# The MLP's first two blocks split by ScalarE and VectorE, and a final norm that follows the last block row by row

## The chip, the cores and the metric

The kernel runs on one core of one Trainium2 chip, in fp32. The metric is device time in microseconds of one execution; lower is better. The median of three runs of the kernel before is 1596.93 us (1596.89 to 1600.69).

## The reference

One layer of a hybrid decoder: a state-space branch and a retention branch whose gated sum goes through `w_out` to the residual, then an MLP with a squared relu, then a last RMS norm. The change touches only what is computed from here on (x, z and h are 1024 x 1024, `w_up` is 1024 x 4096, `w_down` is 4096 x 1024), and every root of an RMS norm:

```python
    z = rmsnorm(h, norm_mlp[l])
    h = h + jnp.square(jax.nn.relu(z @ w_up[l])) @ w_down[l]
return rmsnorm(h, norm_final)
```

## The kernel before, in words

Each fp32 product is made of three matmuls of reduced precision: both operands are split in a rounded part `_hi` and a rest `_lo`, and `three` (L625 to L629) issues hi x hi, hi x lo and lo x hi. So every weight and activation has to be cast (hi) and subtracted (lo) by some engine before TensorE (PE) can use it. Weights come by SP's queue into `stage`, two buffers of 128 x 1024; nothing is loaded into a buffer until its last content has been split.

The 4096 hidden columns are worked off in 16 blocks of 256. The first two (`plain_block`, f = 0 and 1) are plain: four up tiles of 24 matmuls (two column blocks q for each half of the rows) and then 16 down tiles of 6 matmuls, each of them one row chunk c by one half j of the columns, added by VectorE (DVE) from the four banks of `acc` to `h_res` (L2044). The other 14 (`win_block`) use seven half-size up products into `aux` in place of eight, with sums of quarters of the activations (`s1_sum` to `s4_sum`, made by DVE in `form_s1` to `form_s4`, split by ScalarE (ACT) and DVE in `lo_s`) in the gaps of the plain blocks.

What sets the order is each engine's own program and the counters between engines. In a plain block ACT takes relu of up tile n (L1358) and only then makes the `hid_hi` of tile n - 1; DVE squares `relu` (L2055), waits for `hid_hi`, makes `hid_lo` (L1421), and does the sums between these steps. Down tile n waits until tile n - 4 has been added to `h_res` (`out_free`), since there are four banks; the fifth down tile also waits for the last two `hid_lo`. GpSimd (POOL) splits the weights of both plain blocks (`plain_split`, L549 and L551): those of f = 1 once the four up tiles of f = 0 are done. Then it makes the first pieces of block 0's transformed weights as soon as the up tiles of f = 1 are done.

The last block's down products go, as in all blocks, first through all eight rows with j = 0 and then with j = 1 (`DOWN_ORDER` is 4, 5, 6, 7, 0, 1, 2, 3), so a row of `h_res` is complete only in the second half. ACT sums its squares (L1404), DVE takes the roots of rows 0 to 3 together, then of 4 and 5, then of 6 and 7 (`last_rstd`, `rstd`), and multiplies with the root and `nf` (`last_norm`, L2151) in rows 0, 2, 4, 6, 7; rows 1, 3, 5 are scaled by ACT (L1410) and multiplied with `nf` by POOL (L620). SP stores the rows in order, 512 KB each. `nf` lies in `stage` and is loaded (L467) when the last weights have been split. In `rstd` the root is a shift of the bits and three Newton steps on a column or a few; every dependent step waits for the one before (`link`). A root of one column uses TENSOR_SCALAR with two pointer operands, one of several columns TENSOR_TENSOR.

## Time and profile before

| | us |
|---|---|
| median of three runs | 1596.93 |
| the profiled execution | 1595.84 |
| its span in the profile | 1594.0 |
| PE busy | 1516.0 (95%) |
| DVE busy | 955.1 (60%) |
| POOL busy | 434.1 (27%) |
| ACT busy | 292.9 (18%) |
| TensorE's mean granted clock | 0.984 |

In the 40 slices of the profile (39.85 us each) PE stands at 9 tenths from the third slice on but for four slices at 8, one at 6 and the last at 4. The 6 is the slice from 916.6 to 956.4 us, where the plain blocks lie; the last one holds the final norm. In the chain that ended last PE has 84%, DVE 10%, SP's queue 2%. A shown matmul duration of 0.39 us is not its share of the engine, since matmuls overlap: what counts is the distance between starts.

### The profile page before, as it was taken

To read this page: it belongs to the slowest core of one execution; us is meant where nothing else is said; L and a number is where in the kernel's file an instruction comes from. 1 tells how busy PE (TensorE), PEld (TensorE's weight loads), DVE (VectorE), ACT (ScalarE), POOL (GpSimd) and SP (SyncE) were. 2 spreads that over 40 slices of the span, in tenths; PEclk is the share of its full clock that TensorE was granted. 3 is DMA by queue.
4 is the path that set the end of the run, shared out by engine and by line. 5 is a ranking of instruction groups with operands and counts; after the bars stand their busy time and mean duration, and the time that the engine had idled before them with its cause. 6 is when DMAs were issued, how large, how long until landed. Compare 5 with 4: busy or idle time off the path is not lost.

```text
span 1594.0 us, 21227 instructions
## 1 busy us (share of the span) xinstructions
PE 1516.0 (95%) x7440; PEld 1267.6 (80%) x7440; DVE 955.1 (60%) x1928; ACT 292.9 (18%) x569; POOL 434.1 (27%) x363
## 2 busy tenths in 40 slices
PE   5898999899999999999999968999999999999994
PEld 4786888789898989878888756888888888888884
DVE  6688656553565646575516686655555555555557
ACT  4121111210222222241102212111111111111113
POOL 1210101321010101105323133344444444444442
PEclk9999999999999999999999989999999999999997
DMA  5423434354110101104442010111111111111113
GB/s 165 121 93 99 124 98 125 106 192 146 47 54 26 53 26 41 39 27 137 160 158 66 1 53 1 53 53 53 53 53 53 53 53 46 47 52 53 53 40 118
DMA packets 105604, 119.17 MB, mean 75 GB/s; under 512 B 23504, under 2 KB 73808, under 8 KB 105552
## 3 DMA queue, kind: packets, MB, share of 16 engines
q1 hardware_dynamic: 74704, 78.49, 16.1%
q10 hardware_dynamic: 30848, 40.00, 8.0%
q8 instruction: 32, 0.52, 0.1%
q14 instruction: 20, 0.16, 0.0%
HBM read 96.57 MB, written 20.97 MB: 74 GB/s over the span
## 4 chain that ended last, share of the span: by engine, by line
PE 84%; DVE 10%; SPq 2%; ACT 1%; ACTq 1%; DMA 1%; issue 1%; POOL 0%; DVEq 0%
PE acc L627 21%; PE acc L629 20%; PE acc L628 20%; PE aux L629 6%; PE aux L627 6%; PE aux L628 6%; SPq L393 1%; PE aux L871 1%; PE aux L865 1%; PE aux L874 1%; DMA stage<-in_w_in 1%; PE aux L758 1%; ACTq L1127 1%; DVE tb L1734 1%; PE aux L764 0%
## 5 line engine op out<-in xcount | busy, mean ns | idle before, releaser
L2044 DVE TENSOR_TENSOR h_res<-h_res,acc 128x512 f32<-128x512 f32 x256 | 170.8, 685 | 109.5 <-PE acc L629 108.3
L627 PE MATMUL acc<-dw_hi,hid_hi 128*128 128x512 f32 x512 | 201.1, 393 | 19.7 <-DVE h_res L2044 19.7
L629 PE MATMUL acc<-dw_hi,hid_lo 128*128 128x512 f32 x512 | 200.6, 392 | 0.0
L628 PE MATMUL acc<-dw_lo,hid_hi 128*128 128x512 f32 x512 | 200.6, 392 | 0.0
L627 PE MATMUL acc<-w_hi,z_hi 128*128 128x256 f32 (+1 forms) x512 | 189.0, 369 | 0.0
L627 PE MATMUL acc<-z_hi,w_hi 128*128 128x512 f32 x448 | 179.5, 401 | 9.7 <-DVE z_lo L1421 5.0
L502 POOL CAST w_hi<-stage 128x1024 fp32r<-128x1024 f32 x44 | 48.6, 1121 | 494.3 <-PE acc L629 323.4
L628 PE MATMUL acc<-z_lo,w_hi 128*128 128x512 f32 x448 | 176.5, 394 | 0.0
L629 PE MATMUL acc<-z_hi,w_lo 128*128 128x512 f32 x448 | 176.4, 394 | 0.0
L629 PE MATMUL acc<-w_hi,z_lo 128*128 128x256 f32 (+1 forms) x512 | 173.0, 338 | 0.0
L628 PE MATMUL acc<-w_lo,z_hi 128*128 128x256 f32 (+1 forms) x512 | 172.8, 338 | 0.0
L627 PEld LDWEIGHTS acc<-dw_hi,hid_hi 128*128 128x128 f32 x512 | 97.0, 190 | 41.7 <-DVE h_res L2044 21.0
L2093 DVE TENSOR_TENSOR tmp<-tmp,aux 128x512 f32<-128x512 f32 x84 | 57.3, 683 | 103.4 <-PE aux L629 103.4
L629 PEld LDWEIGHTS acc<-dw_hi,hid_lo 128*128 128x128 f32 x512 | 96.9, 189 | 20.3
L628 PEld LDWEIGHTS acc<-dw_lo,hid_hi 128*128 128x128 f32 x512 | 97.1, 190 | 20.0
L627 PEld LDWEIGHTS acc<-z_hi,w_hi 128*128 128x128 f32 x448 | 85.4, 191 | 30.3 <-DVE z_lo L1421 5.8
L629 PEld LDWEIGHTS acc<-w_hi,z_lo 128*128 128x128 f32 x512 | 97.0, 189 | 10.8
L628 PEld LDWEIGHTS acc<-w_lo,z_hi 128*128 128x128 f32 x512 | 97.4, 190 | 8.1
L627 PEld LDWEIGHTS acc<-w_hi,z_hi 128*128 128x128 f32 x512 | 97.2, 190 | 8.2
L629 PEld LDWEIGHTS acc<-z_hi,w_lo 128*128 128x128 f32 x448 | 85.3, 190 | 18.4
L628 PEld LDWEIGHTS acc<-z_lo,w_hi 128*128 128x128 f32 x448 | 85.5, 191 | 17.2
L582 POOL TENSOR_TENSOR t_lo<-stage,t_hi 128x512 fp32r<-128x512 f32 x70 | 91.9, 1313 | 5.6
(300 smaller groups left out, 2839.5 us busy)
## 6 DMA issues: line engine op xcount, KB each, us to landing
stage<-in_w_up SPq DMA_DIRECT2D x32, 512.0 KB, 3.9
stage<-in_w_down SPq DMA_DIRECT2D x32, 512.0 KB, 3.4
stage<-in_w_in SPq DMA_DIRECT2D x28, 512.0 KB, 4.4
gate_dram<-gate_t ACTq DMA_DIRECT2D x32, 256.0 KB, 2.0
x_in<-in_x SPq DMA_DIRECT2D x8, 512.0 KB, 8.2
stage<-in_w_in SPq DMA_DIRECT2D x32, 128.0 KB, 2.7
stage<-in_w_in SPq DMA_DIRECT2D x16, 256.0 KB, 3.2
gb_t<-gate_dram ACTq DMA_DIRECT2D x16, 256.0 KB, 3.0
```

The lines of the kernel that those rows point to most:

```text
L393: sp.dma_start(coef[rows, i, :], t[name][0, gp::2, :].rearrange("g p -> p g"), allow_slow_non_contiguous=True).then_inc(lam_in, 16)
L502: nc.gpsimd.tensor_copy(dst_hi, stage[:, s, :]).then_inc(hi_pool, 1)
L582: nc.gpsimd.tensor_tensor(t_lo[:, slot, :, :], src, t_hi[:, slot, :, :].bitcast(F32), ALU.subtract)\
L627: nc.tensor.matmul(out, s_hi, m_hi_, start=first, stop=False)
L628: nc.tensor.matmul(out, s_hi, m_lo_, start=False, stop=False)
L629: return nc.tensor.matmul(out, s_lo, m_hi_, start=False, stop=last)
L758: nc.tensor.matmul(aux[:, 2 + gp, q * P:(q + 1) * P], toep[:, gp * QP + q, :], u_blk[:, 2 * q + gp, :], start=(q == 0), stop=False)
L865: nc.tensor.matmul(aux[:, 3, 0:DV], kvk[:, c % 2, :], vv[:, c % 2, :], start=True, stop=True)
L871: mm = nc.tensor.matmul(aux[:, 2, 0:DV], prob[:], vv[:, c % 2, :], start=True, stop=(c == 0))
L874: mm = nc.tensor.matmul(aux[:, 2, 0:DV], qkt[:, 0, :], state[:], start=False, stop=True)
L2044: V.tensor_tensor(h_res[:, c, hs], h_res[:, c, hs], acc[:, p % 4, :], ALU.add)\
L2093: V.tensor_tensor(dst, src, aux[:, bank, :], ALU.add).then_inc(taken, 1)
```

## The change

It has four parts.

- **Second block's weights.** The weights of f = 1 are cast by ACT (`second_hi`) and subtracted by DVE (`second_lo`), at fixed places of their programs, with the counters `second_cast` and `second_ready`; POOL splits only those of f = 0. SP's loads that followed POOL's splits follow `second_ready`.
- **Order in the plain blocks.** ACT makes `hid_hi` of tile n right after its relu. DVE makes the sums in another order: `form_s3(1)` moves to f = 1, the two `lo_s` of s3 move from ahead of the down products to among them.
- **The last block.** Its down products go row by row, both halves of a row one after the other; `dw` of j = 1 is split before the last two hidden tiles. DVE only adds, and takes roots in pairs of rows with the instructions of the two interleaved (`pair_rstd`); POOL multiplies rows 0 to 6 with `nf`, ACT scales them; DVE does row 7 in two halves, one stored by SP and one by ACT's queue. PE's and ACT's loops end one block earlier, with the last block written out behind them.
- **Roots.** Every root takes its first guess from the bits of the halved negative value, which saves one instruction.

```diff
+ROOT_BITS = 1597463007.0 - 2.0 ** 22 - 2.0 ** 30
...
+                    if f == 1:
+                        sp.wait_ge(second_ready, j + 1)
+                        sp.dma_start(stage[:, j, :].rearrange("p (k c) -> p k c", k=FT),
+                                     w_dn[:, FT * f:FT * f + FT, j * HALF:(j + 1) * HALF]).then_inc(raw[j], 16)
+                    else:
+                        load(LD_MLP + 4 * f + 2 + j, w_dn[:, FT * f:FT * f + FT, j * HALF:(j + 1) * HALF])
...
-                        sp.wait_ge(w_ready, LD_MLP + 4 * N_PLAIN - 1 + i)
+                        sp.wait_ge(second_ready, 3 + i)
...
-            for p, c in enumerate(DOWN_ORDER):
-                if p % 2 == 0 or p == NCH - 1:
-                    sp.wait_ge(f_done, (p + 1) // 2 + 1)
-                else:
-                    sp.wait_ge(f_done_pool, p // 2 + 1)
+            for p, c in enumerate(DOWN_ORDER[:-1]):
+                sp.wait_ge(f_scaled, p + 1)
                 sp.dma_start(out_rows[:, c, :], h_res[:, c, :]).then_inc(stored, 16)
-            sp.wait_ge(stored, 16 * NCH)
+            sp.wait_ge(f_done, 1)
+            sp.dma_start(out_rows[:, DOWN_ORDER[-1], 0:HALF], h_res[:, DOWN_ORDER[-1], 0:HALF]).then_inc(stored, 16)
+            sp.wait_ge(stored, 16 * (NCH + 1))
...
-            for f in range(N_PLAIN):
-                pool.wait_ge(out_ready, OUT_MLP - 8 if f == 0 else OUT_MLP + 4)
-                for i in range(2):
-                    n = LD_MLP + 4 * f + i
-                    plain_split(n, flat(pw_hi[:, KH * i:KH * i + KH, :]), flat(pw_lo[:, KH * i:KH * i + KH, :]), n + 1)
-                for j in range(2):
-                    n = LD_MLP + 4 * f + 2 + j
-                    if f > 0:
-                        pool.wait_ge(out_ready, OUT_MLP + PLAIN_OUT * (f - 1) + 4 + 8 * (j + 1))
-                    plain_split(n, flat(dw_hi[:, j, :, :]), flat(dw_lo[:, j, :, :]), n + 1)
+            pool.wait_ge(out_ready, OUT_MLP - 8)
+            for i in range(2):
+                n = LD_MLP + i
+                plain_split(n, flat(pw_hi[:, KH * i:KH * i + KH, :]), flat(pw_lo[:, KH * i:KH * i + KH, :]), n + 1)
+            for j in range(2):
+                n = LD_MLP + 2 + j
+                plain_split(n, flat(dw_hi[:, j, :, :]), flat(dw_lo[:, j, :, :]), n + 1)
...
-            for p, c in enumerate((DOWN_ORDER[1], DOWN_ORDER[3], DOWN_ORDER[5])):
-                pool.wait_ge(f_scaled, p + 1)
+            for p, c in enumerate(DOWN_ORDER[:-1]):
+                pool.wait_ge(f_ss, p + 1)
...
+            def down_rows(n0, h0, waits, order):
+
+                for p, c in enumerate(order):
+                    for j in range(2):
+                        down_tile(n0, 2 * p + j, p, c, j, h0, waits)
...
-                    if n >= 1:
-                        hidden_hi(4 * f + n - 1, relu[:, (n - 1) % 2, :], (n - 1) % FT, (n - 1) // FT)
-                hidden_hi(4 * f + 3, relu[:, 1, :], 1, 1)
+                    hidden_hi(4 * f + n, relu[:, n % 2, :], n % FT, n // FT)
+
+            def second_hi(i, dst):
+
+                act.wait_ge(raw[i % 2], 16 * (LD_RET // 2 + HEADS + (LD_MLP - LD_PB) // 2 + 2 + i // 2 + 1))
+                nc.scalar.activation(dst, stage[:, i % 2, :], ACT.Copy).then_inc(second_cast, 1)
 
             plain_block(0)
+            for i in range(2):
+                second_hi(i, pw_hi[:, KH * i:KH * i + KH, :].rearrange("p k c -> p (k c)"))
             for u in range(2):
                 s_hi(3 + u, s2_hi[:, 2 * u:2 * u + 2, :], s2_sum[:, 2 * u:2 * u + 2, :])
+            for j in range(2):
+                act.wait_ge(out_ready, OUT_MLP + 4 + 8 * (j + 1))
+                second_hi(2 + j, dw_hi[:, j, :, :].rearrange("p k c -> p (k c)"))
+            plain_block(1)
...
+                s_hi(5 + 2 * u, s3_hi[:, 2 * u:2 * u + 2, :], s3_sum[:, 2 * u:2 * u + 2, :])
...
+                    if last and i == 1:
+                        dw_hi_part(g, 1)
+                if not last:
+                    dw_hi_part(g, 1)
...
+            def square_f(p):
+                act.wait_ge(out_free, OUT_WIN + 16 * (N_WIN - 1) + 2 * p + 2)
                 if p >= 1:
                     act.wait_ge(f_ss, p)
-                nc.scalar.activation(h_junk[:], h_res[:, c, :], ACT.Square, accum_out=ss2[:, p:p + 1])\
+                nc.scalar.activation(h_junk[:], h_res[:, DOWN_ORDER[p], :], ACT.Square, accum_out=ss2[:, p:p + 1])\
                   .then_inc(f_ss, 1)
-                for s, after in ((1, 4), (3, 5), (5, 7)):
-                    if p == after:
-                        r = DOWN_ORDER[s]
-                        act.wait_ge(f_rstd, 1 if s < 4 else 2)
-                        nc.scalar.activation(h_res[:, r, :], h_res[:, r, :], ACT.Copy, scale=rs2[:, s:s + 1])\
-                          .then_inc(f_scaled, 1)
+
+            def scale_f(p):
+                act.wait_ge(f_done_pool, p + 1)
+                act.wait_ge(f_rstd, p // 2 + 1)
+                nc.scalar.activation(h_res[:, DOWN_ORDER[p], :], h_res[:, DOWN_ORDER[p], :], ACT.Copy,
+                                     scale=rs2[:, p:p + 1]).then_inc(f_scaled, 1)
+
+            for p in range(4):
+                square_f(p)
+            scale_f(0)
+            scale_f(1)
+            square_f(4)
+            square_f(5)
+            scale_f(2)
+            scale_f(3)
+            square_f(6)
+            square_f(7)
+            scale_f(4)
+            scale_f(5)
+            scale_f(6)
+            act.wait_ge(f_done, 2)
+            act.dma_start(out_rows[:, DOWN_ORDER[-1], HALF:D], h_res[:, DOWN_ORDER[-1], HALF:D]).then_inc(stored, 16)
...
-                bits, (tmp, m, y, y2) = rs_bits[:, 0:w], [rs_tmp[:, i, 0:w] for i in range(4)]
-                V.tensor_scalar(m, a, -0.5 / width, -0.5 * EPS, ALU.mult, ALU.add)
-                link(V.tensor_scalar(tmp, a, 1.0 / width, EPS, ALU.mult, ALU.add))
-                link(V.tensor_scalar(bits, tmp.bitcast(I32), 1, None, ALU.arith_shift_right))
-                link(V.tensor_scalar(y.bitcast(I32), bits, -1.0, 1597463007.0, ALU.mult, ALU.add))
+                bits, (m, y, y2) = rs_bits[:, 0:w], [rs_tmp[:, i, 0:w] for i in range(3)]
+                link(V.tensor_scalar(m, a, -0.5 / width, -0.5 * EPS, ALU.mult, ALU.add))
+                link(V.tensor_scalar(bits, m.bitcast(I32), 1, None, ALU.arith_shift_right))
+                link(V.tensor_scalar(y.bitcast(I32), bits, -1.0, ROOT_BITS, ALU.mult, ALU.add))
...
-                    if f == 1 and n < 2:
-                        form_s4(n)
-                    if f == 1 and n >= 2:
+                    if f == 1 and n == 0:
+                        second_lo(3, dw_lo[:, 1, :, :], dw_hi[:, 1, :, :])
+                        form_s4(0)
+                    if f == 1 and n == 1:
+                        form_s3(1)
+                    if f == 1 and n == 2:
+                        form_s4(1)
+                    if f == 1 and n == 3:
                         for u in range(2):
-                            lo_s(2 * n + u - 3, (s2_hi, s3_hi)[n - 2], (s2_lo, s3_lo)[n - 2],
-                                 (s2_sum, s3_sum)[n - 2], u)
+                            lo_s(1 + u, s2_hi, s2_lo, s2_sum, u)
                 for j, p in down(n0 + 4, range(NCH)):
-                    if f == 0 and j == 0 and p == 3:
+                    if f == 0 and j == 0 and p in (1, 3):
+                        ks = slice(KH * (p // 2), KH * (p // 2) + KH)
+                        second_lo(p // 2, pw_lo[:, ks, :], pw_hi[:, ks, :])
+                    if f == 0 and (j, p) == (0, 7):
                         form_s2(1)
-                    if f == 0 and (j, p) in ((0, 7), (1, 3)):
-                        form_s3(j)
-                    if f == 1 and j == 0 and p in (2, 5):
-                        lo_s1(p // 4)
+                    if f == 0 and (j, p) == (1, 3):
+                        form_s3(0)
+                    if f == 0 and (j, p) == (1, 6):
+                        second_lo(2, dw_lo[:, 0, :, :], dw_hi[:, 0, :, :])
+                    if f == 1 and j == 0 and p in (1, 3):
+                        lo_s(3 + p // 2, s3_hi, s3_lo, s3_sum, p // 2)
+                    if f == 1 and j == 0 and p in (5, 7):
+                        lo_s1(p // 2 - 2)
                     if f == 1 and j == 1 and p in (2, 5):
                         lo_s(7 + p // 4, s4_hi, s4_lo, s4_sum, p // 4)
+
+            def second_lo(i, dst, hi):
+                dve.wait_ge(second_cast, i + 1)
+                V.tensor_tensor(dst.rearrange("p k c -> p (k c)"), stage[:, i % 2, :],
+                                hi.rearrange("p k c -> p (k c)").bitcast(F32), ALU.subtract).then_inc(second_ready, 1)
...
+                if last:
+                    dw_lo_part(g, 1)
...
+            def last_rows(n0):
+
+                for p, c in enumerate(DOWN_ORDER):
+                    for j in range(2):
+                        i = 2 * p + j
+                        dve.wait_ge(out_ready, n0 + i + 1)
+                        hs = slice(j * HALF, (j + 1) * HALF)
+                        V.tensor_tensor(h_res[:, c, hs], h_res[:, c, hs], acc[:, i % 4, :], ALU.add).then_inc(out_free, 1)
+                    if p in (2, 4, 6):
+                        pair_rstd(p - 2)
+                pair_rstd(6)
+                dve.wait_ge(f_rstd, 4)
+                c = DOWN_ORDER[-1]
+                for j in range(2):
+                    hs = slice(j * HALF, (j + 1) * HALF)
+                    V.scalar_tensor_tensor(out=h_res[:, c, hs], in0=h_res[:, c, hs], scalar=rs2[:, 7:8], in1=nf[:, hs],
+                                           op0=ALU.mult, op1=ALU.mult).then_inc(f_done, 1)
+
+            def pair_rstd(p):
+
+
+                dve.wait_ge(f_ss, p + 2)
+                two = [(ss2[:, i:i + 1], rs2[:, i:i + 1], rs_bits[:, i - p:i - p + 1],
+                        [rs_tmp[:, k, i - p:i - p + 1] for k in range(3)]) for i in (p, p + 1)]
+                (a0, d0, b0, (m0, y0, t0)), (a1, d1, b1, (m1, y1, t1)) = two
+                V.tensor_scalar(m0, a0, -0.5 / D, -0.5 * EPS, ALU.mult, ALU.add)
+                link(V.tensor_scalar(m1, a1, -0.5 / D, -0.5 * EPS, ALU.mult, ALU.add))
+                V.tensor_scalar(b0, m0.bitcast(I32), 1, None, ALU.arith_shift_right)
+                link(V.tensor_scalar(b1, m1.bitcast(I32), 1, None, ALU.arith_shift_right))
+                V.tensor_scalar(y0.bitcast(I32), b0, -1.0, ROOT_BITS, ALU.mult, ALU.add)
+                link(V.tensor_scalar(y1.bitcast(I32), b1, -1.0, ROOT_BITS, ALU.mult, ALU.add))
+                for step in range(3):
+                    V.tensor_scalar(t0, y0, y0, m0, ALU.mult, ALU.mult)
+                    link(V.tensor_scalar(t1, y1, y1, m1, ALU.mult, ALU.mult))
+                    V.tensor_scalar(d0 if step == 2 else y0, t0, 1.5, y0, ALU.add, ALU.mult)
+                    ins = V.tensor_scalar(d1 if step == 2 else y1, t1, 1.5, y1, ALU.add, ALU.mult)
+                    ins.then_inc(f_rstd, 1) if step == 2 else link(ins)
```

## Rows read from the trace of the kernel before

**Rows 1.** Windows: PE, PEld, DVE, ACT, POOL busy (instructions), granted clock, DMA share, GB/s.
```profile
1043.00:1570.00 527.00, 527.00 (x2324) 436.04 (x2323) 303.41 (x427) 71.19 (x98) 227.46 (x224) 1.00 0.16 51
1570.00:1575.00 5.00, 3.84 (x17) 2.84 (x16) 4.59 (x16) 2.62 (x5) 0.84 (x1) 1.00 0.00 0
```

**Rows 2.** Timeline of PE: start, duration, engine, line, operation [idle before <-releaser].
```profile
928.01 0.80 PE L627 MATMUL acc<-dw_hi,hid_hi 128*128 128x512 f32 x1 [10.32 <-DVE h_res L2044]
...
943.26 0.50 PE L627 MATMUL acc<-dw_hi,hid_hi 128*128 128x512 f32 x1 [1.99 <-DVE h_res L2044]
...
984.23 0.80 PE L627 MATMUL acc<-dw_hi,hid_hi 128*128 128x512 f32 x1 [7.43 <-DVE h_res L2044]
```

**Rows 3.** Timeline of DVE in the first plain block.
```profile
908.00 0.69 DVE L1421 TENSOR_TENSOR hid_lo<-tmp,hid_hi 128x512 fp32r<-128x512 f32 x1 [4.09 <-ACT hid_hi L1039]
...
909.86 1.23 DVE L2004 TENSOR_TENSOR s_part<-m_lo 128x1024 f32<-128x1024 f32 x1
...
914.32 3.41 DVE L2003 TENSOR_TENSOR s_sum<-m_hi 128x1024 f32<-128x1024 f32 x1
...
919.74 3.25 DVE L2005 TENSOR_TENSOR s_sum<-s_sum,s_part 128x1024 f32<-128x1024 f32 x1
...
927.28 2.47 DVE L2044 TENSOR_TENSOR h_res<-h_res,acc 128x512 f32<-128x512 f32 x4
```

**Rows 4.** Timeline of POOL in the same stretch, the last of four operations.
```profile
918.70 3.20 POOL L551 TENSOR_TENSOR pw_lo<-stage,pw_hi 128x1024 fp32r<-128x1024 f32 x1
```

**Rows 5.** Windows behind idle stretches of PE, columns as in rows 1; then its timeline.
```profile
928.00:932.40 4.40, 4.39 (x10) 3.51 (x11) 4.37 (x6) 0.67 (x2) 0.00 (x0) 0.50 0.00 0
943.26:947.26 4.00, 4.00 (x18) 3.31 (x19) 3.97 (x5) 0.44 (x1) 0.00 (x0) 1.00 0.04 14
703.70:707.30 3.60, 3.60 (x10) 2.83 (x9) 3.25 (x13) 0.00 (x0) 0.00 (x0) 0.53 0.00 0
285.00:289.00 4.00, 4.00 (x49) 3.76 (x49) 0.00 (x0) 0.00 (x0) 0.79 (x1) 1.00 0.44 130
...
703.37 0.50 PE L627 MATMUL acc<-z_hi,w_hi 128*128 128x512 f32 x1 [2.59 <-DVE z_lo L1421]
```

**Rows 6.** Timeline of DVE in the second plain block, before its down products.
```profile
973.27 3.85 DVE L2030 TENSOR_TENSOR s_lo<-s_sum,s_hi 128x1024 fp32r<-128x1024 f32 x2
...
979.74 3.84 DVE L2030 TENSOR_TENSOR s_lo<-s_sum,s_hi 128x1024 fp32r<-128x1024 f32 x2
983.50 1.87 DVE L2044 TENSOR_TENSOR h_res<-h_res,acc 128x512 f32<-128x512 f32 x3
```

**Rows 7.** Timeline of DVE: the steps of one root of one column.
```profile
9.10 0.15 DVE L1435 TENSOR_SCALAR rs_tmp<-ss 128x1 f32<-128x1 f32 x1
9.16 0.14 DVE L1436 TENSOR_SCALAR rs_tmp<-ss 128x1 f32<-128x1 f32 x1
...
9.72 0.27 DVE L1442 TENSOR_SCALAR rs_tmp<-rs_tmp 128x1 f32<-128x1 f32 x1
10.03 0.21 DVE L1443 TENSOR_SCALAR rs_tmp<-rs_tmp 128x1 f32<-128x1 f32 x1
```

**Rows 8.** Timelines of ACT and DVE in the final norm; the last is SP's landing time.
```profile
1565.08 1.06 ACT L1404 ACTIVATE h_junk<-h_res 128x1024 bf16<-128x1024 f32 x1 [9.97 <-DVE h_res L2044]
...
1588.38 2.48 DVE L2151 SCALAR_TENSOR_TENSOR h_res<-h_res,rs,stage 128x1024 f32<-128x1024 f32 x2
...
stage<-in_norm_final SPq DMA_DIRECT2D x1, 512.0 KB, 3.6
```

**Rows 9.** Timelines of POOL and DVE, where both are at work.
```profile
846.18 2.39 POOL L551 TENSOR_TENSOR dw_lo<-stage,dw_hi 128x1024 fp32r<-128x1024 f32 x1
...
846.59 0.27 DVE L1442 TENSOR_SCALAR rs_tmp<-rs_tmp 128x1 f32<-128x1 f32 x1
...
1578.24 2.34 POOL L620 TENSOR_TENSOR h_res<-h_res,stage 128x1024 f32<-128x1024 f32 x1 [0.69 <-ACT h_res L1410]
...
1578.28 2.32 DVE L1446 TENSOR_TENSOR rs_tmp<-rs_tmp 128x2 f32<-128x2 f32 x1
```

More of the change, by code:

```diff
@@ L964, in _, with down_tile @@
                         turn_z2(c - 2)
+            def down_tile(n0, i, p, c, j, h0, waits):
+                pe.wait_ge(out_free, n0 + (i - 3))
+                if j == 0 and p % 4 == 0:
+                    pe.wait_ge(lo_done, h0 + 2 + p // 2)
+                if p == 0:
+                    pe.wait_ge(*waits[j])
+                for q in range(FT):
+                    mm = three(acc[:, i % 4, :], hid_hi[:, q, c * P:(c + 1) * P],
+                               hid_lo[:, q, c * P:(c + 1) * P], dw_hi[:, j, q, :], dw_lo[:, j, q, :],
+                               q == 0, q == FT - 1)
+                mm.then_inc(out_ready, 1)
             def down(n0, h0, waits, order):
@@ L1001, in plain_block, with win_block @@
                         mm.then_inc(out_ready, 1)
-                down(n0 + 4, SP_HID + 4 * f, [(w_ready, LD_MLP + 4 * f + 3 + j) for j in range(2)], range(NCH))
-            def win_block(g, first):
+                down(n0 + 4, SP_HID + 4 * f, [(w_ready, LD_MLP + 3 + j) if f == 0 else (second_ready, 3 + j) for j in range(2)], range(NCH))
+            def win_block(g, first, last=False):
                 a = {"A11": (m_hi[:, 0:KH, 0:HALF], m_lo[:, 0:KH, 0:HALF]),
@@ L1025, in win_block @@
                     mm.then_inc(prod, 1)
-                down(g * 16 + OUT_WIN, g * 4 + (SP_HID + 4 * N_PLAIN), [(dn_ready, g * 2 + (1 + j)) for j in range(2)],
-                     DOWN_ORDER)
+                (down_rows if last else down)(g * 16 + OUT_WIN, g * 4 + (SP_HID + 4 * N_PLAIN),
+                                              [(dn_ready, g * 2 + (1 + j)) for j in range(2)], DOWN_ORDER)
             for f in range(N_PLAIN):
@@ L1376, in _, with win_block @@
                   .then_inc(s_cast, 1)
[L1378 removed]
+            def win_block(g, last=False):
                 h0 = g * 4 + 4 * N_PLAIN
@@ L2143, in last_rstd @@
[L2143 to L2152 removed]
+                for _ in down(g * 16 + OUT_WIN, DOWN_ORDER):
+                    pass
```

61 lines of the change are left out of this document (16 added, 45 removed).

## The prediction

> **What bounds the kernel now.** I read the page first: TensorE (PE) is busy for 95% of the span and has 84% of the chain that ended last, so only time in which PE stands or runs slowly counts. The windows by stage come next. From 1043 to 1570 us, in the transformed blocks, PE starts 2324 matmuls in 527.0 us without a gap and at full clock, one per 0.227 us; a down tile of six thus takes 1.36 us and an up tile of 24 takes 5.45 us [rows 1]. Nothing is to be had there. PE's timeline then shows what the change can reach. In the first plain block PE stands 10.32 us ahead of its fifth down tile and 1.99 us further on; in the second block it stands 7.43 us at the same place [rows 2]. Each time the releaser is the addition to `h_res` by VectorE (DVE). The last place is behind PE's end: 3.84 of the 5 us from 1570 on are busy, so PE ends at about 1573.8 and 20.2 us of span follow [rows 1].
>
> DVE's timeline says why the addition is late. It has not begun adding: it starts at 927.28 and goes through four at once, 0.61 us each [rows 3]. Ahead of that lie the sums. One operation of 128x1024 takes 1.23 us while POOL rests, but the three of `form_s1(1)` take from 914.32 to 922.99, that is 8.67 us [rows 3], just while POOL splits the second block's weights, its own subtraction lengthened to 3.20 us [rows 4]. And `hid_lo` of tile 1 waited 4.09 us for a cast that ScalarE (ACT) gives only after the next tile's relu [rows 3].
>
> **First plain block.** Without POOL's splits `form_s1(1)` takes 3 x 1.25 = 3.75 us: 4.9 us go. ACT's cast right after its relu brings `hid_lo` of tile 1 from 908.0 to about 904.6: its wait of 4.09 shrinks to the 0.7 us that one cast and its handing over take. What follows in DVE's order (one sum, square, cast, `hid_lo`) moves up by the same 3.3 us. The additions start 8.2 us earlier, and the stall of 10.32 becomes 2.1. Late next is again the first addition, now behind `form_s2(0)`.
>
> TensorE's clock: behind the 10.32 us of idle time it was granted at 0.50, the lower level of 1.2 GHz, and ten matmuls took 4.40 us in place of 2.27 [rows 5], so 2.1 us more are lost. Behind 1.99 us of idle time it stayed at full speed [rows 5]. At the length that remains the trace has both: the matmuls behind the wait at 285 us ran at full clock, those behind 2.59 us of idle time at 703 us had 0.53 for ten matmuls, a loss of 3.60 - 2.27 = 1.3 us [rows 5]. I take no fall here.
>
> The splits move to ACT and DVE: four casts of about 1.1 us on ACT, which is idle most of the time, and four subtractions of 1.23 us on DVE. Three of these and two sums (2.5 and 3.75 us) share the 16 down tiles with 16 additions of 0.61: 9.8 + 3.7 + 6.2 = 19.7 us of DVE work under 21.8 us of PE work. With four banks an addition may be about 3.5 us late before PE waits; the longest insertion is `form_s3(0)`, 3.75 us, with DVE less than a microsecond behind then, so at most some tenths. The 1.99 us stall goes, since the second `form_s3` has left this block, and so does a wait of 0.3 at its end. The second block's first weights are ready in the middle of these tiles, some 12 us before PE wants them. Behind ACT's waits are queued only its casts for s2, which nobody needs before the second block. SP's loads wait for `second_ready` in place of POOL: 3 to 4 us of landing against more than 15 of cover. Gain of the first block: 8.2 + 2.1 + 2.0 + 0.3 = 12.6 us.
>
> **Second plain block.** Before, the square of the last hidden tile waited for two `lo_s` that took 3.85 us [rows 6], and POOL was making its first pieces all the time; two more `lo_s` (3.84) stood between `hid_lo` and the additions at 983.50 [rows 6]. The first two are moved among the down tiles; in their place the last operation of `form_s4(1)` reaches into the stretch with POOL, about 1.9 us. POOL starts its pieces at the same point relative to PE, so the latter two `lo_s` stay slow. The stall goes from 7.43 to 3.6 us. Its bounds: if DVE suffers nothing from POOL it would be 0.7, if everything is lengthened as in the first block (8.67 for 3.75) 5.5. I take 3.6, since the nearest rows are the same operations beside the same POOL work [rows 6]. After that much I let the clock fall as before, so its cost stays. The `lo_s` between the down tiles cost a few tenths at full clock and nothing while PE is slow. Gain 3.8 us, bounds 1.9 and 8.2 (the latter with the clock kept). Together 16.4 us.
>
> **The last block.** Row by row, a row of `h_res` is complete every 2.73 us rather than in the second half, so squares, roots, products and stores start about 8 us earlier. What bounds is DVE. Its pair of roots is 18 operations of one column. The trace shows two independent ones 0.06 us apart, and a dependent one 0.31 behind an operation with two pointers [rows 7]; an interleaved pair of two pointer operations is not in it. Bounds: with 0.06 throughout it is 2.9 us, with no overlap at all 4.5. I take 3.4, adding to 0.06 the 0.12 by which an operation with pointers is longer than one without [rows 7]. In two rows DVE then has 4 x 0.61 + 3.4 = 5.8 us of work in PE's 5.45, so it falls a little behind, and the third root stands ahead of the last two additions.
>
> I laid the four programs side by side from these durations: square 1.06 + 0.2 and its reading [rows 8], scaling 1.15, POOL's product 2.34 [rows 9]. `nf` is requested when the last `dw` is split, at about 1552.8, and lands 3.6 us later [rows 8], so DVE's first addition is at 1556.5, as before (1556.3); PE doesn't feel it. The second half's `dw` is just ready when the second tile wants it (0 to 0.3 us). Tile 14 waits 0.5 us for its bank. The last addition ends at 1577.8, the last square at 1579.2, the last pair of roots at 1582.7, ACT's scaling of row 6 and DVE's two halves at 1584.0. Before, the last row but one was complete at 1589.66 (the first half of the 2.48 us [rows 8]), and the rest of the span from there, 4.3 us, was two stores of 512 KB. Now the same megabyte becomes ready at once at 1584.0 to 1584.1, so the span would end at 1588.4 by the old clock: a gain of 5.6 us, with 7 at the short root and 2 at the long one.
>
> POOL now works through these rows without much rest. Two rows say what that does. A DVE operation of two columns that started 0.04 us after POOL's product took 2.32 us, as long as POOL's 2.34; one of one column ran in its usual 0.27 us within a subtraction of POOL [rows 9]. The pairs are of one column, so I let them pass. [...]
>
> **All roots.** One instruction less, an independent one that was issued 0.06 us after its neighbour [rows 7]. On PE's path only at the start, at the ends of the branches and before the MLP: 0 to 0.4 us, I take 0.1. The loops that end one block earlier cost nothing in sight: block 0 is written out already, and PE has no gap from there on [rows 1].
>
> **Sum.** 12.6 + 3.8 + 5.6 + 0.1 = 22.1 us from the profiled execution's 1595.84: 1573.7. The runs' median lies 1.1 above that execution, so the forecast is 1574.8.
>
> **Rivals.**
> 1. POOL isn't what made the sums slow, or DVE meets something else there: the first stall keeps 4.9 us and with them the fall of the clock (2.1), and the second keeps 1.9. Gain 13.2, time 1583.7. Against it: the same operations at 1.23 wherever POOL rests. 8%.
> 2. Everything falls well: the second stall is 0.7 to 1.5, the clock stays up, roots are short. Gain 26 to 28, time about 1570. 14%.
> 3. One-column operations do wait for POOL, in the last block. Four products of 2.35 lie beside the first three roots: 9.4 us more on DVE, which is the bound, and the tail ends 3.8 us later than before in place of 5.6 earlier: 1584.2. 5%.
> 4. Slower than before: with its rests gone PE is not granted full clock through the 14 transformed blocks. They take 567 us at 1.00 now; 22 us are eaten when the mean falls below 0.962, and at 0.95 the time is 1605. For it is only that the clock is seen at 0.50 and 0.53 in places; but these are behind idle time, and 527 us without a rest ran at 1.00 [rows 1, 5]. 2%.
> 5. The last block's new order stalls PE (banks or `dw`), some 3 to 6 us: 1579. 8%.
>
> The forecast's own case has 63%, 1570 to 1579.
>
> **How the numbers follow.** The range reaches from the low bounds (12.6 + 8.2 + 7 + 0.4 is 28.2, so 1568.7) to the high ones with a second fall of the clock (10.8 + 1.9 + 2 is 14.7, so 1582.2); I give 1568.5 to 1582, which leaves out rivals 3 and 4 and part of 1. This kernel's measurements tell about 0.3%, 4.8 us, from no change. Only rival 4 gives slower, 2%; within 0.3% needs the sum of several misses, 1%; faster 97%.
>
> **What the profile would show.** First block: `form_s1(1)` near 3.75 us and a PE wait of 2 to 2.5 ahead of the fifth down tile, no second one, and 12.6 us less up to the second block. Second: a wait of 3 to 4 with the clock at 0.5 behind it. Last: pairs of roots of 3.4 us that don't change with POOL, PE at most 1 us late, and 14 to 15 us from PE's end to the end of the span. The prediction is wrong if one of the waits is made by something else than DVE's additions, if one-column operations lengthen to POOL's durations, or if the clock in the transformed blocks isn't 1.00.

## The result and the profile after

The changed kernel takes 1575.35 us in the median of four runs (1573.48 to 1579.54), the kernel before 1596.91 (1596.12 to 1600.69). The ratio is 0.9864, with a 95% interval of 0.9839 to 0.9889. The forecast was 1574.8 us. The profiled execution took 1576.09 us, 19.75 less than before's, with a mean granted clock of 0.987; the sum of the prediction had 22.1 less.

The page of after, in the lines that answer to the table of before:

```profile
span 1574.2 us, 21201 instructions
...
PE 1516.3 (96%) x7440; PEld 1269.3 (81%) x7440; DVE 946.2 (60%) x1918; ACT 300.9 (19%) x577; POOL 426.8 (27%) x359
```

PE's busy time is what it was, so slow stretches cost it as much as before; 20 us of standing still are gone. Where from is read by cutting both programs at the same matmuls (starts from PE's timeline, in us; the last down products go to the start of the last matmul, and its own 0.39 us stands in neither of the last two rows):

| stretch | before | after | gain | predicted |
|---|---|---|---|---|
| up to the third up tile of block 0 | 901.06 | 902.80 | -1.74 | 0.1 (roots) |
| its last two up tiles | 11.03 | 11.02 | 0.01 | |
| first block's 16 down tiles | 37.22 | 24.03 | 13.19 | 12.6 |
| second block's up tiles | 21.89 | 21.76 | 0.13 | |
| second block's down tiles | 30.80 | 28.69 | 2.11 | 3.8 |
| transformed blocks | 549.88 | 549.64 | 0.24 | 0 |
| last down products | 21.58 | 22.47 | -0.89 | -0.5 to -0.8 |
| PE's end to the end of the span | 20.15 | 13.40 | 6.75 | 5.2 to 6.2 |

The windows of after give the same stretches (span; busy time and count of PE, PEld, DVE, ACT, POOL; granted clock, DMA share, GB/s). They answer to [rows 1]:

```profile
913.82:937.85 24.03, 22.07 (x98) 17.95 (x96) 22.56 (x27) 6.19 (x7) 0.00 (x0) 1.00 0.14 44
959.61:988.30 28.69, 24.42 (x97) 19.69 (x96) 25.38 (x27) 7.14 (x8) 14.72 (x9) 0.88 0.00 1
969.50:976.00 6.50, 6.50 (x18) 5.19 (x19) 6.31 (x8) 0.00 (x0) 5.46 (x4) 0.61 0.01 3
988.30:1537.90 549.60, 549.60 (x2425) 455.27 (x2424) 315.43 (x443) 71.43 (x97) 245.72 (x242) 1.00 0.17 52
1537.94:1560.80 22.86, 22.22 (x97) 17.76 (x95) 19.35 (x65) 11.09 (x17) 13.43 (x6) 1.00 0.19 70
1560.80:1574.20 13.40, 0.00 (x0) 0.00 (x0) 7.23 (x31) 5.92 (x8) 3.24 (x2) 0.66 0.60 235
```

96 down matmuls at full speed take 96 x 0.2267 = 21.76 us. The first block is 2.3 us above that, the second 6.9. PE's timeline shows the waits that are left, all for DVE's additions as before [rows 2]:

```profile
921.38 0.50 PE L631 MATMUL acc<-dw_hi,hid_hi 128*128 128x512 f32 x1 [1.96 <-DVE h_res L2086]
...
969.47 0.80 PE L631 MATMUL acc<-dw_hi,hid_hi 128*128 128x512 f32 x1 [4.27 <-DVE h_res L2086]
...
1544.18 0.50 PE L631 MATMUL acc<-dw_hi,hid_hi 128*128 128x512 f32 x1 [0.64 <-DVE h_res L2204]
```

DVE's timeline ahead of the first two (first block, then second), for [rows 3] and [rows 6], and the first of POOL's pieces:

```profile
906.34 0.69 DVE L1464 TENSOR_TENSOR hid_lo<-tmp,hid_hi 128x512 fp32r<-128x512 f32 x1 [0.70 <-ACT hid_hi L1055]
...
912.60 1.22 DVE L2045 TENSOR_TENSOR s_sum<-m_hi 128x1024 f32<-128x1024 f32 x1
...
915.12 1.23 DVE L2047 TENSOR_TENSOR s_sum<-s_sum,s_part 128x1024 f32<-128x1024 f32 x1
...
920.64 1.28 DVE L2086 TENSOR_TENSOR h_res<-h_res,acc 128x512 f32<-128x512 f32 x2
...
959.76 1.23 DVE L2066 TENSOR_TENSOR s_sum<-s_sum 128x1024 f32<-128x1024 f32 x1
...
959.92 2.21 POOL L594 TENSOR_TENSOR t_sum<-stage 128x512 f32<-128x512 f32 x1 [6.93 <-PE acc L633]
...
960.90 1.78 DVE L2097 TENSOR_TENSOR tmp<-tmp 128x512 f32<-128x512 f32 x1
963.38 1.69 DVE L1464 TENSOR_TENSOR hid_lo<-tmp,hid_hi 128x512 fp32r<-128x512 f32 x1 [0.70 <-ACT hid_hi L1055]
964.99 3.83 DVE L2072 TENSOR_TENSOR s_lo<-s_sum,s_hi 128x1024 fp32r<-128x1024 f32 x2
968.75 1.27 DVE L2086 TENSOR_TENSOR h_res<-h_res,acc 128x512 f32<-128x512 f32 x2
```

`form_s1(1)` takes 3.75 us (912.60 to 916.35) and `hid_lo` of tile 1 waits 0.70 us, both as written. In the second block POOL's first piece starts at 959.92 and the operations of DVE behind it are longer: the square 1.78 where it takes 0.68 without POOL, `hid_lo` 1.69 for 0.69, the two `lo_s` 3.83 for 2.35.

### The profile page after: what moved, and what is told of

Read it like the earlier page. It is cut to its first block, busy times and chain, and to the rows that moved or that the text cites. A ratio compares the mean times of both kernels' runs of the same rounds, so it can differ in the third digit from the quotient of the medians.

```text
span 1574.2 us, 21201 instructions
## 1 busy us (share of the span) xinstructions
PE 1516.3 (96%) x7440; PEld 1269.3 (81%) x7440; DVE 946.2 (60%) x1918; ACT 300.9 (19%) x577; POOL 426.8 (27%) x359
## 4 chain that ended last, share of the span: by engine, by line
PE 83%; DVE 10%; SPq 2%; ACT 1%; ACTq 1%; DMA 1%; issue 1%; POOL 0%; DVEq 0%
PE acc L631 20%; PE acc L633 20%; PE acc L632 20%; PE aux L632 5%; PE aux L633 5%; PE aux L631 5%; SPq L396 1%; PE aux L875 1%; PE aux L869 1%; PE aux L878 1%; PE aux L762 1%; DMA stage<-in_w_in 1%; ACTq L1143 1%; DVE tb L1776 1%; PE aux L768 1%
## 5 line engine op out<-in xcount | busy, mean ns | idle before, releaser
L2086 DVE TENSOR_TENSOR h_res<-h_res,acc 128x512 f32<-128x512 f32 x240 | 160.5, 686 | 101.2 <-PE acc L633 99.9
L591 POOL TENSOR_TENSOR stage<-stage 128x512 f32<-128x512 f32 x14 | 18.2, 1302 | 285.9 <-DMA stage<-in_w_up 285.9
```

What stands on the lines that cost most here:

```text
L591: pc.link(nc.gpsimd.tensor_tensor(b12, b12, b11, ALU.subtract))
L2086: V.tensor_tensor(h_res[:, c, hs], h_res[:, c, hs], acc[:, p % 4, :], ALU.add)\
```

## The experiments

With each run go those of its stretches that bear on the question. "First" and "second" are the down tiles of the two plain blocks, before: 37.22 and 30.80 us with stalls of 10.32 (and 1.99) and 7.43.

**The plain blocks alone, the last block alone.** `e1_mlp` is the kernel before with the change's plain-block and split parts, `e2_last` the kernel before with the new last block; together they are the change, but for the roots outside the last block, which have the old form in both.

> The kernel before with the plain blocks' part alone (weights of the second block by ACT and DVE, new order of casts and sums); last block, final norm and roots as before. Theory (the stalls are DVE's sums, slowed by POOL in the first block): from PE's first matmul behind the m_lo wait to the first transformed block 100.9 us become 85.5 as in the changed kernel: 15.4 us less, with stalls of 2.0 and 4.3 us and the clock at its lower level behind the second. Tail 20.1 us as before. Time about 1581.5. Rival (the gain of the plain blocks leans on the other parts): less than 10 us.

> The kernel before with the last block's part alone (down products row by row, new final norm, pairs of roots); plain blocks and the other roots as before. Theory: PE's last down products take 22.5 us in place of 21.6, because DVE's first addition waits for the norm's weights, and 13.4 us in place of 20.2 follow PE's end: 5.9 us less, time about 1591. Plain blocks with their stalls of 10.3, 2.0 and 7.4 us. Rival (part of the tail's gain is something else, such as the loops that end earlier): more than 1 us away from 5.9.

`e1_mlp`: 1581.86 us (four runs), ratio 0.9909 (0.9892 to 0.9925); stalls of 1.92 and 4.27. `e2_last`: 1591.24 us (five runs), ratio 0.9961 (0.9947 to 0.9975); last down products 22.24, then 13.12 to the end. The ratios compare with the kernel before in runs of the same session. By them the two savings are 14.5 and 6.2 us of about 1597, sum 20.7, each known to some 2.5 us; the change gave 21.7. The parts add up within the spread of the runs, so these runs show no part disturbing the other.

In `e1_mlp` the clock fell behind the wait of 1.92 us, which it did not in the changed kernel behind 1.96. Its window behind that wait:

```profile
919.50:923.80 4.30, 4.30 (x13) 3.38 (x12) 4.19 (x6) 0.00 (x0) 0.00 (x0) 0.60 0.39 129
```

Its first block took 25.58 for 24.03. With that, the stretch from block 0's third up tile to the first transformed block was 87.56 us, 13.4 less than before and not 15.4.

**Is it POOL that lengthens the sums, and does its time matter?** In the kernel before, POOL's splits for f = 1 wait for four down tiles more, so that they no longer meet `form_s1(1)`.

```diff
-                pool.wait_ge(out_ready, OUT_MLP - 8 if f == 0 else OUT_MLP + 4)
+                pool.wait_ge(out_ready, OUT_MLP - 8 if f == 0 else OUT_MLP + 8)
```

> The kernel before with one number changed: POOL begins to split the second block's weights when the fourth down tile of the first block is done, not at the end of its up tiles. Theory (POOL's splits lengthen form_s1(1) from 3.75 to 8.67 us and with it the first stall): form_s1(1) takes 3.75 us, PE's stall ahead of the fifth down tile falls from 10.3 to 5.4 us; POOL's splits then lie beside additions from PSUM and sums further on. Rival (something else makes these three operations slow): the stall stays at 10.3.

The stall stayed: 10.40 us, and the time of the one run was 1596.34. A miss, and an instructive one. The sums did what was expected, but POOL's work (916.91 to 925.5) now met the square, `hid_lo` and `form_s2(0)`:

```profile
913.41 1.22 DVE L2003 TENSOR_TENSOR s_sum<-m_hi 128x1024 f32<-128x1024 f32 x1
...
919.29 2.05 DVE L1421 TENSOR_TENSOR hid_lo<-tmp,hid_hi 128x512 fp32r<-128x512 f32 x1 [0.70 <-ACT hid_hi L1039]
...
923.35 3.25 DVE L2011 TENSOR_TENSOR s_sum<-s_sum,m_lo 128x1024 f32<-128x1024 f32 x1
...
927.25 0.79 PE L627 MATMUL acc<-dw_hi,hid_hi 128*128 128x512 f32 x1 [10.40 <-DVE h_res L2044]
```

The first sum fell from 3.41 [rows 3] to 1.22, `hid_lo` took 2.05 for the 0.69 that it takes elsewhere [rows 3] and the second operation of `form_s2(0)` 3.25 for 1.23. So POOL is the cause of the length (rival 1 of the prediction falls), and what it costs hardly depends on which of DVE's operations it meets, as long as they stand ahead of the additions: from `hid_lo` of tile 2 to the first addition DVE took 13.63 us in the kernel before and 13.72 here, against 8.65 in the changed kernel, where POOL is away. Moving POOL's work by some us inside that stretch gives nothing; it has to leave the stretch, as in the change.

**The hand-over alone.** In the kernel before, ACT casts right after its relu.

```diff
-                    if n >= 1:
-                        hidden_hi(4 * f + n - 1, relu[:, (n - 1) % 2, :], (n - 1) % FT, (n - 1) // FT)
-                hidden_hi(4 * f + 3, relu[:, 1, :], 1, 1)
+                    hidden_hi(4 * f + n, relu[:, n % 2, :], n % FT, n // FT)
```

> The kernel before with one edit: in the plain blocks ACT casts a hidden tile right after its relu. POOL still splits the second block's weights. Theory: hid_lo of tile 1 comes 3.3 us earlier and form_s1(1) begins ahead of POOL's splits, so it is partly undisturbed; the first stall falls by 3.3 us at least and by up to 8; the second stall stays at 7.4, since it starts from the last tile, whose cast already followed its square. Rival (the early cast is covered by other work): no stall changes.

1588.73 us (one run), stalls of 7.02 and 3.34. The first is the 3.3 us of the prediction (10.32 to 7.02). POOL again met other operations, and the same path of DVE took 13.76 us. What is left over the 1.92 of `e1_mlp` is 5.1 us, POOL's part. The second was not to change, and fell by 4.09 us:

```profile
923.21 0.80 PE L627 MATMUL acc<-dw_hi,hid_hi 128*128 128x512 f32 x1 [7.02 <-DVE h_res L2042]
...
965.60 2.35 DVE L2028 TENSOR_TENSOR s_lo<-s_sum,s_hi 128x1024 fp32r<-128x1024 f32 x2
...
968.52 1.29 POOL L590 TENSOR_TENSOR t_sum<-stage 128x512 f32<-128x512 f32 x1 [13.11 <-PE acc L629]
...
972.67 3.83 DVE L2028 TENSOR_TENSOR s_lo<-s_sum,s_hi 128x1024 fp32r<-128x1024 f32 x2
...
977.15 0.76 PE L627 MATMUL acc<-dw_hi,hid_hi 128*128 128x512 f32 x1 [3.34 <-DVE h_res L2042]
```

With the cast earlier, the first pair of `lo_s` runs at 965.60, before POOL's pieces begin (968.52), in 2.35 us in place of 3.85 [rows 6], and in time in which DVE only waited.

**The move of the `lo_s` alone, and the change without it.** That raised a doubt about the reason that the prediction gave for the second block, the move of two `lo_s` to the down tiles. Two kernels decide it: the kernel before with only this move, and the changed kernel with only this move undone.

```diff
-                    if f == 1 and n >= 2:
-                        for u in range(2):
-                            lo_s(2 * n + u - 3, (s2_hi, s3_hi)[n - 2], (s2_lo, s3_lo)[n - 2],
-                                 (s2_sum, s3_sum)[n - 2], u)
+                    if f == 1 and n == 3:
+                        for u in range(2):
+                            lo_s(1 + u, s2_hi, s2_lo, s2_sum, u)
...
-                    if f == 1 and j == 0 and p in (2, 5):
-                        lo_s1(p // 4)
+                    if f == 1 and j == 0 and p in (1, 3):
+                        lo_s(3 + p // 2, s3_hi, s3_lo, s3_sum, p // 2)
+                    if f == 1 and j == 0 and p in (5, 7):
+                        lo_s1(p // 2 - 2)
```

> The kernel before with one thing of the change: in the second plain block the first two lo_s (tile 2) leave their place and the s3 and m_lo ones stand among the down tiles, as in the change; the cast's hand-over stays old. My prediction's reason for 3.8 us was this move. If the move is enough by itself, the square of the last tile starts right behind hid_lo of tile 2, the additions come 3.8 us earlier and the stall is 7.4 - 3.8 = 3.6 us: time 3.8 less, about 1593. If only the earlier hand-over counts (it alone gave 7.43 -> 3.34), the square waits for something else and the stall stays above 6: under 1.5 us less.

> The changed kernel with only that move undone: two lo_s behind form_s4(1), two ahead of the additions; the new hand-over and ScalarE's splits stay. If the hand-over alone would have brought the gain of the second block, its stall stays near 4.3 and the time near 1575. If the move is needed because second_lo(3) and form_s3(1) now fill VectorE up to GpSimd's stretch, the two lo_s run beside GpSimd in 3.8 us and the stall is 4.3 + 3.8 = 8.1 us: 3.8 us more, about 1579.

`e10_move_only` took 1591.61 us where the kernel before, run beside it, took 1595.34; `e11_not_moved` took 1578.29. Each is one run, and runs of one kernel differ by as much, so the stalls decide. PE's timelines, of `e10_move_only` and then of `e11_not_moved`:

```profile
979.90 0.80 PE L627 MATMUL acc<-dw_hi,hid_hi 128*128 128x512 f32 x1 [3.67 <-DVE h_res L2044]
```

```profile
971.81 0.79 PE L631 MATMUL acc<-dw_hi,hid_hi 128*128 128x512 f32 x1 [8.01 <-DVE h_res L2086]
```

And DVE's of `e11_not_moved`, ahead of that wait:

```profile
959.49 3.86 DVE L2072 TENSOR_TENSOR s_lo<-s_sum,s_hi 128x1024 fp32r<-128x1024 f32 x2
963.28 1.75 DVE L2097 TENSOR_TENSOR tmp<-tmp 128x512 f32<-128x512 f32 x1
...
967.32 3.84 DVE L2072 TENSOR_TENSOR s_lo<-s_sum,s_hi 128x1024 fp32r<-128x1024 f32 x2
```

Set side by side, the second block's stall is:

| | `lo_s` ahead of the additions | two of them moved |
|---|---|---|
| before | 7.43 | 3.67 (`e10_move_only`) |
| before, hand-over early | 3.34 (`e5_handoff`) | not run |
| the change (hand-over early, two more steps on DVE) | 8.01 (`e11_not_moved`) | 4.27 |

In the kernel before either edit alone was enough: the move takes the pair out, the hand-over lets it run in free time. In the changed kernel the hand-over's free time is spent on what the change puts there, `second_lo(3)` (1.22) and `form_s3(1)` (2.31 + 1.23 + 1.23), so the move is worth its 3.74 us. The prediction's step stands.

**What is left in the second block.** One number of the changed kernel: POOL begins its first pieces of the transformed weights after the fifth down tile of the second block, not at the end of its up tiles (the counter runs over the four up tiles too).

```diff
-                    pool.wait_ge(out_ready, OUT_MLP + PLAIN_OUT * (N_PLAIN - 1) + 4)
+                    pool.wait_ge(out_ready, OUT_MLP + PLAIN_OUT * (N_PLAIN - 1) + 9)
```

> The changed kernel, with POOL's first pieces of transformed block 0 started once the fifth down tile of the second plain block is done, not at the end of its up tiles (one number). Theory (POOL beside DVE makes the second stall): DVE's square, hid_lo and two lo_s before its first addition take their undisturbed 0.6, 0.6 and 2.4 us, the stall falls from 4.3 to about 1 us and the clock stays up: 5 to 6 us less up to the first transformed block, unless its pieces are late (POOL needs 14 us from about 967, PE wants the first at about 982). Rival (the chain of handing over from ACT to DVE makes the stall): it stays above 3 us.

1570.81 us (four runs), ratio 0.9841 (0.9823 to 0.9859). The second block takes 22.88 us in place of 28.69. DVE's pair of `lo_s` is back at 2.35 us, and PE's wait is short:

```profile
961.35 2.35 DVE L2072 TENSOR_TENSOR s_lo<-s_sum,s_hi 128x1024 fp32r<-128x1024 f32 x2
...
964.36 0.50 PE L631 MATMUL acc<-dw_hi,hid_hi 128*128 128x512 f32 x1 [0.69 <-DVE h_res L2086]
...
958.07:980.95 22.88, 22.19 (x97) 17.77 (x95) 22.15 (x27) 7.14 (x8) 13.08 (x9) 1.00 0.00 1
```

So the whole remaining stall but 0.7 us was POOL's, and most of the 2.66 us by which the block lay above 21.76 + 4.27 was the clock that fell behind it: 18 matmuls took 6.50 us from 969.50 on, where full speed needs 4.08. The first transformed block still found its pieces in time.

**Do one-column roots escape POOL?** The last block of the changed kernel with the interleaved pair replaced by one root over two columns.

```diff
-                two = [(ss2[:, i:i + 1], rs2[:, i:i + 1], rs_bits[:, i - p:i - p + 1],
...
+                rstd(rs2[:, p:p + 2], ss2[:, p:p + 2], D, done=f_rstd)
```

> The changed kernel with each pair of roots of the last block taken by operations of two columns in place of two interleaved one-column operations. Theory (two-column operations of two SBUF sources or one wait for a running POOL operation, one-column ones don't): one or more of the 12 small operations in each of the first three roots last up to 2.3 us, a root beside POOL takes 5 to 7 us in place of 3.3, PE waits for banks, and the last block with its tail takes 6 to 15 us longer than the changed kernel's 35.9. Rival (interleaving merely overlaps latencies, POOL has no part): each root 2.4 us, the block and tail 1 to 3 us shorter.

1583.57 us (one run). The last down products and the tail take 45.05 us in place of 35.87. A pair of roots is 12 instructions there in place of 18, but those that meet POOL (three products in 7.10 us from 1544.16 on) wait for a product to end:

```profile
1546.64 2.32 DVE L1479 TENSOR_SCALAR rs_bits<-rs_tmp 128x2 int32<-128x2 int32 x1
1548.99 2.30 DVE L1480 TENSOR_SCALAR rs_tmp<-rs_bits 128x2 int32<-128x2 int32 x1
1551.33 0.16 DVE L1487 TENSOR_TENSOR rs_tmp<-rs_tmp 128x2 f32<-128x2 f32 x1
...
1553.71 0.80 PE L631 MATMUL acc<-dw_hi,hid_hi 128*128 128x512 f32 x1 [2.97 <-DVE h_res L2204]
```

In the changed kernel the same steps with one column, in the middle of POOL's products:

```profile
1546.05 7.11 POOL L624 TENSOR_TENSOR h_res<-h_res,stage 128x1024 f32<-128x1024 f32 x3 [13.96 <-ACT h_junk L1431]
...
1547.84 0.15 DVE L2222 TENSOR_SCALAR rs_tmp<-ss 128x1 f32<-128x1 f32 x1
...
1548.08 0.15 DVE L2224 TENSOR_SCALAR rs_bits<-rs_tmp 128x1 int32<-128x1 int32 x1
...
1548.58 0.27 DVE L2229 TENSOR_SCALAR rs_tmp<-rs_tmp 128x1 f32<-128x1 f32 x1
1548.77 0.27 DVE L2230 TENSOR_SCALAR rs_tmp<-rs_tmp 128x1 f32<-128x1 f32 x1
...
1551.05 2.47 DVE L2204 TENSOR_TENSOR h_res<-h_res,acc 128x512 f32<-128x512 f32 x4
```

The pair takes 1551.05 - 1547.84 = 3.21 us, and none of its 18 operations is longer than 0.27. This is what makes the new last block possible at all: with two-column roots it takes 45.05 us, more than the 41.73 of the kernel before.

**The wait for the norm's weights.** In the changed kernel DVE waits for `nf` ahead of its first addition, though it multiplies with `nf` only in the last row. The wait goes behind the last pair of roots.

```diff
                 dve.wait_ge(f_rstd, 4)
+                dve.wait_ge(nf_in, 16)
...
-            dve.wait_ge(nf_in, 16)
             last_rows(OUT_WIN + 16 * (N_WIN - 1))
```

> The changed kernel with DVE's wait for the final norm's weights moved from ahead of the last block's additions to ahead of its own two products at the end (POOL keeps its own wait). Theory (that wait holds DVE for 1.95 us and PE for 0.6): PE has no wait in the last down products, 21.6 us in place of 22.5, the tail behind stays at 13.4: 0.6 to 0.9 us less. Rival (PE's wait is cover for DVE's lateness, which comes back in the tail): no less than 0.2.

1579.37 us in its one run, which says nothing by itself: 906.16 us of it lie ahead of block 0's third up tile, 3.4 more than in the changed kernel's profile and untouched by the edit. The stretches compared tell more: last down products 21.53 for 22.47, no wait of PE, and 13.44 for 13.40 behind them. 0.9 us less, as expected.

**All of it.** The pieces later, the wait behind, and in both plain blocks no more than one sum or subtraction between two of DVE's additions: the s2 `lo_s` also stand among the down tiles, and so does `form_s2(0)`, which stood ahead of the first addition.

```diff
-                    if f == 0 and n == 3:
-                        form_s2(0)
...
-                    if f == 0 and (j, p) == (0, 7):
-                        form_s2(1)
-                    if f == 0 and (j, p) == (1, 3):
+                    if f == 0 and (j, p) in ((0, 5), (1, 1)):
+                        form_s2(j)
+                    if f == 0 and (j, p) == (1, 5):
                         form_s3(0)
...
-                    if f == 1 and n == 3:
-                        for u in range(2):
-                            lo_s(1 + u, s2_hi, s2_lo, s2_sum, u)
...
+                    if f == 1 and j == 0 and p in (1, 2):
+                        lo_s(p, s2_hi, s2_lo, s2_sum, p - 1)
```

> The changed kernel with four edits: POOL's first pieces after the fifth down tile of the second block; DVE's wait for the norm's weights moved behind; the two lo_s that stood ahead of the second block's additions spread among its down tiles with the others; form_s2(0) of the first block moved among its down tiles, form_s2(1) and form_s3(0) two tiles later or so. Theory: with nothing but hid_lo between the last hidden tile and the additions both stalls vanish (under 0.5 us each) and the clock never falls in the plain blocks: first block 21.9 to 22.5 us in place of 24.0 to 25.6, second 21.8 to 22.3 in place of 28.7, last down products 0.7 less; about 1567. Rival (the sums moved among the down tiles overfill DVE, 22 us of work in 21.8): stalls of 1 to 3 us come back later in the blocks.

1564.21 us in the median of five runs (1562.48 to 1568.68), ratio 0.9785 (0.9766 to 0.9804): faster than both kernels, and its slowest run is below the fastest of the changed kernel. Both plain blocks run nearly as fast as PE can (21.76 us):

```profile
916.10:937.86 21.76, 21.76 (x97) 18.02 (x96) 20.92 (x26) 6.20 (x7) 0.00 (x0) 1.00 0.15 48
959.62:981.66 22.04, 21.93 (x98) 17.83 (x96) 21.31 (x27) 7.15 (x8) 14.35 (x9) 1.00 0.00 1
```

## Why the prediction was right, point by point

The mechanisms held but for one step of the last block, and every stretch moved the way that was forecast but for the roots' tenth. That the median lies 0.6 us from the forecast is partly luck: the profiled execution gained 19.8 us for 22.1, and the four runs spread over 6 us.

**First block: 12.6 predicted, 13.2 measured.** Both causes are shown apart: the hand-over by `e5_handoff` (3.3 us), POOL by `e4_pool_later` and by the 3.75 us of `form_s1(1)` in the changed kernel. The stall that remains is 1.96 for 2.1, with `form_s2(0)` late next, which `e9_first_too` confirms: without it no stall is left. The choice to let the clock stay up held in the changed kernel's profile and not in `e1_mlp`, so it was a choice between two things that both happen: of the six profiles with this wait three kept the clock (first block 24.0 us) and three did not (25.6). That it came out right is luck.

**Second block: 3.8 predicted, 2.1 measured.** The mechanism stood (`e11_not_moved`: 3.74 us), the sizes of two terms were off. The stall shrank by 3.16, to 4.27 and not 3.6: the prediction let only the last operation of `form_s4(1)` meet POOL, where that one, begun 0.16 us ahead of POOL's piece, kept its 1.23, and the square and `hid_lo` behind it took 1.78 and 1.69 instead, where in the kernel before they had taken 1.09 and 0.98:

```profile
977.05 1.09 DVE L2055 TENSOR_TENSOR tmp<-tmp 128x512 f32<-128x512 f32 x1
...
978.84 0.98 DVE L1421 TENSOR_TENSOR hid_lo<-tmp,hid_hi 128x512 fp32r<-128x512 f32 x1 [0.70 <-ACT hid_hi L1039]
```

The other 1.05 us is the clock. "I let the clock fall as before, so its cost stays" took the cost for constant; beyond stall and full speed the block had 30.80 - 21.76 - 7.43 = 1.61 us before and 28.69 - 21.76 - 4.27 = 2.66 after: 6 matmuls at half speed in before, 11 in after, and 14 behind the same wait in `e1_mlp`. The first of these errors is one of placing: POOL's cost was tied to operations that the rows of before happened to show beside it, where it goes with the stretch of time.

**Last block: 5.6 predicted, 5.9 measured.** The pair of roots took 3.21 for 3.4, beside POOL and without. PE's end to the end of the span took 13.4 for 14 to 15. PE was late by 0.9 us, in the predicted size but for another reason: of the arrival of `nf` the prediction said "PE doesn't feel it", and this step failed. `nf` took longer to land than in [rows 8], and DVE's first addition waited for it:

```profile
1543.43 3.13 DVE L2204 TENSOR_TENSOR h_res<-h_res,acc 128x512 f32<-128x512 f32 x5 [1.95 <-DMA stage<-in_norm_final]
...
stage<-in_norm_final SPq DMA_DIRECT2D x1, 512.0 KB, 4.6
```

The 0.5 us that tile 14 was to wait for its bank did not come: with the wait for `nf` gone, PE has no wait at all in these tiles (`e7_nf_wait`). One term too many and one too few happened to cancel.

**Roots: 0.1 predicted, not measurable.** The stretch ahead of block 0's third up tile took between 899.53 and 906.28 us in the six profiles with the old form of the root there, and between 898.89 and 906.16 in the six with the new one. A tenth can't be seen in that. Of the 1.74 us that after lost there, 1.4 lie behind one wait at 285 us, where its clock fell and that of before did not (last section); they are no effect of the change that these runs could show.

**The rivals.** POOL not being the cause falls by `e4_pool_later`. The transformed blocks ran at 1.00 for 549.60 us, so the clock's rival falls (with the last down products they took 571.5 us before, not the 567 of that rival; nothing hangs on it). The last block's order cost PE 0.9 us and not 3 to 6, and the second stall was 4.27 and not 0.7 to 1.5, so neither of these two rivals came. That one-column operations wait for POOL falls by the rows above, and what two columns would have cost is now measured: 9.2 us, close to the 9.4 that the prediction gave as the bound for waits in the one-column form.

The Trainium skill (VectorE: DVE Perf Modes, section What auto-detection actually checks) has an operation with a single source use both read ports where the outermost non-unit dimensions of source and destination, both in SBUF, are even or equal. Two columns meet that; one column has no such dimension, and the section does not say what holds for it. The rows do: beside a running product of POOL 128x1 took 0.15 and 0.27 us, as elsewhere, and 128x2 took 2.32, until the product ended. That a port is what two columns wait for is shown by no run here.

## What to carry to other kernels

Work of GpSimd cost VectorE about the same wherever the two met ahead of the operation that the chain waits for (5.0 to 5.1 us in three placements of the same splits), so take it out of that stretch (to an idle engine, or behind it) rather than shift it within. Between the additions that free TensorE's banks put at most one long operation, and place the rest among them early; a wait that goes may give back 1.3 to 3.0 us of clock beside its own length, or nothing. And ask of every wait at the head of a stage which instruction really needs it: here the first addition waited for the weights of the last row.

## What the hardware showed that was not expected

**The clock behind short waits is not decided by their length.** Behind eleven waits of PE between 1.92 and 1.99 us in the plain blocks of these kernels, at the same two places of the same programs, the granted clock fell in four (`e1_mlp`, `e3_two_col`, `e6_pieces_later`, `e5_handoff`) and stayed at 1.00 in seven (both kernels, `e2_last`, `e4_pool_later`, `e10_move_only`, `e11_not_moved`, `e7_nf_wait`). Some 200 us earlier all twelve profiles have a wait of 2.59 us, the one of [rows 5] at 703 us, and there it is the other way round: the clock stayed up in those four and fell in those seven (and in `e9_first_too`, which has no later wait of this kind). So the two places are hardly independent. Behind the waits of the first 20 us (3.1 to 3.2, and 9.3 to 10.3) the clock stayed at 1.00; after that it fell behind every wait of 3.3 us or more, and behind none between 0.9 and 1.71. At 285 us one wait shows both; the 16 small matmuls behind it took, in before and in after:

```profile
284.96 2.05 PE L758 MATMUL aux<-u_blk,toep 128*128 128x128 f32 x16 [2.78 <-DVE hst L1742]
```

```profile
285.49 3.44 PE L762 MATMUL aux<-u_blk,toep 128*128 128x128 f32 x16 [2.75 <-DVE hst L1784]
```

A fall cost between 1.3 and 3.0 us in these waits, 6 to 14 matmuls started 0.43 us apart in place of 0.23. It is one source of the several us by which runs of the same kernel differ, and not the only one: in these programs, which are alike up to there but for the form of the root, the wait at 285 us itself lasted 1.53 us in six profiles, 2.68 to 2.78 in three and 5.11 to 5.20 in three (`e2_last`, `e7_nf_wait`, `e9_first_too`), which are the three with the longest stretch ahead of the plain blocks (905.05 to 906.28 us). What tips the clock, and what lengthens that wait, stays open.

**How much interleaving two chains of one column gives.** A pair takes 3.21 us, 0.18 for each of 18 operations, where two roots one after the other would take 4.5 (one root of this form takes 2.24 at the start of the same profile, from 9.14 to 11.38). The starts in one of its three steps are 1548.58, 1548.77, 1549.07, 1549.20 and 1549.44: 0.19 and 0.13 us between the two chains, but 0.30 and 0.24 to the next operation of the first chain, about the distance of a dependent one in the kernel before [rows 7]. The code links the second operation of each two, so the first chain's next waits for the second chain as well; about half of the latency is hidden, not all. A kernel with a link of its own for each chain was not run.
